# RWKV chunk scan: half of each group's heads cross between the partition halves, so that a product uses all four 64x64 squares of the array

## The chip, the cores and the metric

One core of one Trainium2 chip. The metric is the device time of one launch in microseconds (us). TensorE (PE in the profile) multiplies; VectorE (DVE), ScalarE (ACT) and GpSimd (POOL) work on elements; SyncE (SP) issues most of the loads.

## The reference, cut to what matters

The whole model is several layers; the change touches only the last mixer, an RWKV-7 scan over 16 heads of width 64, run forward and backward over 256 context tokens and 256 latent tokens:

```
S_t = S_{t-1} (diag(w_t) - kk_t^T (a_t * kk_t)) + v_t^T k_t
y_t = S_t r_t
```

All inputs and outputs are float32. `y_t` is wanted for the latent tokens only; each direction starts its latent tokens from the state that its context tokens left.

## The kernel before, in words

The scan goes in chunks of 64 tokens: 8 chunks forward (rounds 0 to 7), then 8 backward (rounds 8 to 15), and round 16 only finishes. Inside a chunk everything is a product of 64x64 blocks, one for each head: cumulated decays (`cum`), the masked products between keys and values (`lta`, `mt`, `rab`), the inverse of a unit triangular matrix by doubling and joining (`n2`, `n3`, `n4`, `p`, `f0`, `m2`, `q2`, `m3`, `q3`), and the values with the state (`w`, `t1`, `t2`, `us`, `s`, `y`). `rab` and `y` exist in latent chunks only (`late`), `s` and `fab` not in the last chunk of a direction (`feeds`).

The 16 heads are in two groups g of 8 heads. A tile of a group is [128, 4, 64]: block a (0 to 3) and partition half i (0 or 1) are a head, so that one tile holds 8 heads. `quarters` issues for one product 8 matmuls (times the number of terms): for each a, half 0 then half 1. Head (a, i) has both operands on partitions 64i to 64i+63, and its result goes to the same half. In the array that is square (0,0) and square (1,1), in turn; squares (0,1) and (1,0) are used by `cum` alone. In the trace each float32 matmul is two MATMUL records with a LDWEIGHTS each, so that a product of 8 matmuls has 16 records.

Each engine runs a generator for each group (`scan_pe`, `scan_act`, `scan_dve`, `scan_pool`). A round has ten steps, one for each yield, here called step 0 to 9. `lead` puts group 0 five steps ahead, and then the two take turns, so that every engine's queue is in a fixed order: step k of group 0, step k-5 (modulo 10) of group 1, and so on. In step 0 of round n stand `cum` of n and `w` of round m = n-1; 1: `t1`; 2: `lta`, `t2`; 3: `n2`, `us`; 4: `n3`, `n4`, `s`, `y`; 5: `p`; 6: `f0`, `m2`; 7: `q2`, `mt`; 8: `m3`, `fab`; 9: `q3`, `rab`. The chunk's own chain goes through all of them; each result is taken out of PSUM by ACT (`BY_ACT`) or DVE before the next step's product reads it. A `Line` makes every instruction of ACT, DVE and POOL wait for the one before it on its engine.

Each group has four of the eight PSUM banks, in rotation over its products (`bank_no`); `T.bank` waits until the product that had the bank four products ago has been taken out.

## Time and profile before

| what | value |
|---|---|
| median of 3 runs | 2984.02 us (2983.59 to 2987.77) |
| the profiled execution, own time | 2979.91 us |
| its span | 2978.1 us |
| mean granted TensorE clock | 0.972 |
| PE busy | 2831.3 us (95%) |
| DVE, ACT, POOL busy | 1742.9, 1296.3, 112.2 us |

A matmul's record lasts from its start to the modelled end of its result, and records overlap; the rate of a stream of matmuls is read from the starts (or from a stretch's length over its count), not from the mean length of a record. The clock is a share of 2.4 GHz, so that 0.50 is the lower level of 1.2 GHz.

### The profile page before, as it was taken

The page shows a single profiled execution, that of the slowest core. Times are in us where ns is not written, and L with a number is a line of the kernel's source. Part 1 is how long each engine was busy: PE and PEld are TensorE (multiplying, and loading weights), DVE is VectorE, ACT ScalarE, POOL GpSimd, SP SyncE. Part 2 cuts the span into 40 slices and gives each one's busy share as a digit, 9 for nine tenths or more (in the row PEclk, how much of TensorE's full clock was granted, in tenths as well). Part 3 has the DMA queues.
Part 4 walks back from the last instruction along what each step waited for, and adds up shares of the span by engine and source line. Part 5 has one row for each costly group of instructions (what it writes and reads, how often), then busy time and mean ns, then how long its engine had stood idle before and what let it go on. Part 6 is the DMA issues. An engine that isn't in the chain of part 4 may idle for free.

```text
span 2978.1 us, 63232 instructions
## 1 busy us (share of the span) xinstructions
PE 2831.3 (95%) x26684; PEld 2314.0 (78%) x26684; DVE 1742.9 (59%) x2702; ACT 1296.3 (44%) x2044; POOL 112.2 (4%) x152
## 2 busy tenths in 40 slices
PE   8999999999999999998989999998999999998998
PEld 7887788888877888676758777784547998985986
DVE  6756667586565765213466877545324564565885
ACT  6645566465555665222435332334104434433333
POOL 0000000000000000000000000000001222220000
PEclk9999999999999999997989999999999999999999
DMA  6554345555543554431001433311210000002443
GB/s 256 187 184 164 134 170 185 180 189 191 188 156 119 186 189 153 176 144 60 2 10 57 169 143 142 120 68 64 99 43 3 5 5 25 5 4 114 156 142 113
DMA packets 50409, 349.72 MB, mean 117 GB/s; under 512 B 5840, under 2 KB 5840, under 8 KB 9808
## 3 DMA queue, kind: packets, MB, share of 16 engines
q1 hardware_dynamic: 49680, 343.56, 32.5%
q8 instruction: 212, 3.47, 0.5%
q0 software_dynamic: 448, 2.11, 0.2%
q14 instruction: 69, 0.57, 0.1%
HBM read 344.61 MB, written 1.05 MB: 116 GB/s over the span
## 4 chain that ended last, share of the span: by engine, by line
PE 82%; DVE 11%; ACT 3%; issue 2%; DMA 1%; DVEq 0%; ACTq 0%; SPq 0%
PE psum L165 81%; DVE arena L98 2%; DVE ring_low L87 2%; DVE arena L87 2%; DVE wide L87 2%; PE psum L170 1%; ACT w_high L144 1%; DVE wide L98 1%; DVE ring L87 1%; DMA ring<-in_evt 1%; ACT wide L138 0%; ACT arena L144 0%; ACT arena L140 0%; ACT L138 0%; DVE small L106 0%
## 5 line engine op out<-in xcount | busy, mean ns | idle before, releaser
L165 PE MATMUL psum<-x_both,w_high 128*128 128x512 f32 (+1 forms) x2800 | 845.1, 374 | 10.4 <-DVE arena L87 8.2
L87 DVE TENSOR_TENSOR ring_low<-ring,w_high 128x2048 fp32r<-128x2048 f32 (+3 forms) x254 | 560.3, 2206 | 427.4 <-ACT w_high L144 412.7
L144 ACT ACTIVATE w_high<-ring 128x2048 fp32r<-128x2048 f32 (+3 forms) x254 | 469.5, 1848 | 528.6 <-PE psum L165 236.5
L165 PE MATMUL psum<-x_both,ring_low 128*128 128x256 f32 (+1 forms) x2104 | 605.3, 301 | 0.0
L165 PEld LDWEIGHTS psum<-x_both,w_high 128*128 128x128 f32 x2800 | 494.9, 190 | 107.2 <-issue 17.6
L165 PE MATMUL psum<-w_high,x_both 128*128 128x512 f32 (+2 forms) x1440 | 451.8, 390 | 10.6 <-issue 10.0
L165 PEld LDWEIGHTS psum<-x_both,ring_low 128*128 128x128 f32 x2104 | 398.3, 189 | 32.5 <-DVE x_both L98 1.4
L165 PE MATMUL psum<-wide,ring 64*64 64x64 f32 (+3 forms) x3888 | 383.6, 272 | 12.4 <-DVE wide L87 7.4
L165 PEld LDWEIGHTS psum<-wide,ring 64*64 64x64 f32 (+2 forms) x3888 | 269.1, 147 | 108.3 <-issue 78.2
L165 PEld LDWEIGHTS psum<-w_high,x_both 128*128 128x128 f32 x1440 | 276.3, 195 | 74.9 <-issue 21.5
L165 PE MATMUL psum<-ring_low,x_both 128*128 128x512 f32 (+2 forms) x720 | 278.7, 387 | 0.0
L144 ACT ACTIVATE arena<-psum 128x256 f32<-128x256 f32 (+1 forms) x341 | 148.4, 435 | 212.3 <-PE psum L165 185.3
L165 PE MATMUL psum<-wide 64*64 64x64 f32 (+3 forms) x5808 | 208.2, 218 | 6.6 <-issue 1.9
L98 DVE SCALAR_TENSOR_TENSOR arena<-arena,prm 128x256 f32<-128x256 f32 x396 | 192.1, 485 | 14.1
L165 PEld LDWEIGHTS psum<-wide 64*64 64x64 f32 (+2 forms) x5808 | 184.7, 133 | 17.8 <-issue 6.8
L165 PE MATMUL psum<-w_high,h_high 128*128 128x512 f32 x440 | 172.4, 392 | 4.1 <-DVE ring_low L87 4.1
L165 PE MATMUL psum<-w_high,h_low 128*128 128x512 f32 x440 | 171.4, 390 | 0.0
L165 PE MATMUL psum<-ring_low,h_high 128*128 128x512 f32 x440 | 171.4, 390 | 0.0
L144 ACT ACTIVATE wide<-psum 128x256 f32<-128x256 f32 (+3 forms) x223 | 102.2, 459 | 146.3 <-PE psum L165 134.5
L87 DVE TENSOR_TENSOR arena<-arena,psum 128x256 f32<-128x256 f32 (+1 forms) x240 | 112.3, 468 | 84.6 <-ACT arena L144 62.7
L165 PEld LDWEIGHTS psum<-ring_low,x_both 128*128 128x128 f32 x720 | 140.8, 196 | 24.9
L165 PE MATMUL psum<-ring,wide 64*64 64x64 f32 (+2 forms) x2016 | 147.5, 238 | 1.5 <-issue 0.8
(201 smaller groups left out, 3022.0 us busy)
## 6 DMA issues: line engine op xcount, KB each, us to landing
ring<-in_f_gu SPq DMA_DIRECT2D x88, 1024.0 KB, 4.9
ring<-in_w_mod SPq DMA_DIRECT2D x48, 1024.0 KB, 4.9
ring<-in_fu SPq DMA_DIRECT2D x44, 1024.0 KB, 4.8
ring<-in_f_dn SPq DMA_DIRECT2D x40, 1024.0 KB, 4.9
ring<-in_w_in SPq DMA_DIRECT2D x28, 1024.0 KB, 4.9
ring<-in_fd SPq DMA_DIRECT2D x20, 1024.0 KB, 4.8
ring<-in_rkvr SPq DMA_DIRECT2D x12, 1024.0 KB, 4.8
ring<-in_w_out SPq DMA_DIRECT2D x8, 1024.0 KB, 5.0
```

The lines of the kernel that those rows point to most:

```text
L87: self.done(self.eng.tensor_tensor(o, a, b, op), then)
L98: self.done(self.eng.scalar_tensor_tensor(out=o, in0=a, scalar=s, in1=b, op0=op0, op1=op1), then)
L144: self.done(self.eng.activation(o, i, ACT.Copy, scale=scale), then)
L165: ins = self.eng.matmul(o, l, r, start=a, stop=z)
L170: ins = self.eng.transpose(o, i, ident[0:i.shape[0], 0:i.shape[0]])
```

## The change

- Blocks a = 0 and 1 of a tile stay as they are. For a = 2 and 3 a product of two operands on half i puts its result on half 1-i (`cross`, `head`). The order is now: squares (0,0), (1,1), (0,1), (1,0), then the same for the next pair of blocks.
- Each cross product moves blocks 2 and 3 to the other half. A product whose inputs and result must have the same side uses the old way (`straight`): `p`, `q3`, one half of `q2`, and the term with the state in `w` and `y`. In `w`, `y` and `q2` it writes to the PSUM bank that a cross product has just written, and PE waits for that one before blocks 2 and 3 (`behind`).
- `n2` gets a third product (the identity minus the near block, turned), because its copy on the other side is now needed; ACT takes three blocks out at once. `it` on DVE is half as wide. `f0` is in `m2`'s banks.
- A product has two banks: blocks 0, 1 in the first, blocks 2, 3 in the second. A group therefore has only two places, chosen by name (`SECOND`), and `T.pair` waits until the product last put there has been taken out.
- `s`, `y`, `mt`, `rab`, `fab` and the moments of the output stand in other steps: `y` in 5, `s` in 6, `rab` in 7, `mt` in 8, `fab` in 9. `pc` is now an Exp on ACT in place of a copy on DVE.
- `value_rows` puts the values into the new layout with the same number of copies.

```diff
+    def pair(self, b, tick):
+        for t in self.taken[b] + tuple(t for t in self.taken[b + 1] if t not in self.taken[b]):
+            self.eng.wait_ge(*t)
+        self.taken[b] = self.taken[b + 1] = (tick,)
 
     def mm(self, o, l, r, a, z, then=None):
...
 
-        STFT, SIT, SUT, SATB, SRAB, SKA, SRH = [[blocks(2) for _ in TWO] for _ in range(7)]
+        SUT = [unit(3).rearrange("p (y k t) -> p y k t", y=3, k=4) for _ in TWO]
+        STFT, SATB, SRAB, SKA, SRH = [[blocks(2) for _ in TWO] for _ in range(5)]
         SE1 = [unit(2)[:, 0:264].rearrange("p (k t) -> p k t", k=4) for _ in TWO]
-        SAL, SBE, SE2, SLT, SMJ, SM4, STD, SMT, SWW, SUS = [[blocks() for _ in TWO] for _ in range(10)]
+        SAL, SBE, SE2, SLT, SMJ, SM4, STD, SMT, SWW, SUS, SIT = [[blocks() for _ in TWO] for _ in range(11)]
         ST = unit(2).rearrange("p (k v) -> p k v", k=8)
 
         MIXES = (4, 2, 1, 5, 0, 3)
...
-        bank_no = [{key: 4 * g + n % 4 for n, key in enumerate(order_of)} for g in TWO]
-
-        def scan_bank(g, key):
-            return bank(bank_no[g][key])
-
-        def single(g, key):
-            return scan_bank(g, key)[:, 0:256].rearrange("p (k t) -> p k t", k=4)
+        SECOND = ("w", "lta", "n2", "n3", "p", "m2", "q2", "m3", "q3")
+
+        def first_bank(g, key):
+            return 4 * g + 2 * (key[1] in SECOND)
+
+        def blocks_of(g, key):
+
+            b = first_bank(g, key)
+            return psum[:, b:b + 2, :].rearrange("p b n -> p (b n)").rearrange("p (k y t) -> p y k t", k=4, y=4)
+
+        def single(g, key, y=0):
+            return blocks_of(g, key)[:, y]
 
         def double(g, key):
-            return scan_bank(g, key).rearrange("p (y k t) -> p y k t", y=2, k=4)
+            return blocks_of(g, key)[:, 0:2]
 
...
@@ -2963,36 +2973,60 @@
             te = T.eng
             al, be, mj, mj4, td, mt, ww, us = [x[g] for x in (SAL, SBE, SMJ, SM4, STD, SMT, SWW, SUS)]
             tt_, tf = STFT[g][:, 0], STFT[g][:, 1]
-            itt = SIT[g][:, 0]
-            uu, tq = SUT[g][:, 0], SUT[g][:, 1]
+            it1 = SIT[g]
+            uu, tq, itt = [SUT[g][:, y] for y in range(3)]
             mm, a_, d_, p_ = sc_mm[g], sc_a[g], sc_d[g], sc_p[g]
 
             def take(key):
-                T.bank(bank_no[g][key], a_[key[0], BY_ACT[key[1]]] if key[1] in BY_ACT else d_[key])
-
-            def quarters(o, terms, then=None):
+                T.pair(first_bank(g, key), a_[key[0], BY_ACT[key[1]]] if key[1] in BY_ACT else d_[key])
+
+            def head(o, l, r, a, i, j, begin, end, then=None):
+
+                p, q = slice(64 * i, 64 * i + 64), slice(64 * j, 64 * j + 64)
+                T.mm(o[q, a, :], l[p, a, :], r[p, a, :] if len(r.shape) == 3 else r[p, :], begin, end, then)
+
+            def cross(o, terms, then=None, open_=False):
+
+                for k, (l, r) in enumerate(terms):
+                    for a in TWO:
+                        end = k == len(terms) - 1 and a == 1 and not open_
+                        for b in (a, a + 2):
+                            for i in TWO:
+                                last = k == len(terms) - 1 and b == 3 and i
+                                head(o, l, r, b, i, 1 - i if b > 1 else i, k == 0 and a == 0, end, then if last else None)
+
+            def straight(o, l, r, begin, then=None, behind=None):
 
                 for a in FOUR:
-                    for k, (l, r) in enumerate(terms):
-                        for i in TWO:
-                            p = slice(64 * i, 64 * i + 64)
-                            T.mm(o[p, a, :], l[p, a, :], r[p, a, :] if len(r.shape) == 3 else r[p, :], k == 0,
-                                 k == len(terms) - 1, then if a == 3 and k == len(terms) - 1 and i else None)
+                    if a == 2 and behind:
+                        te.wait_ge(*mm[behind])
+                    for i in TWO:
+                        head(o, l, r, a, i, i, begin and a % 2 == 0, a % 2 == 1, then if a == 3 and i else None)
 
             def one(key, *terms):
                 take(key)
-                quarters(single(g, key), terms, mm(key))
+                cross(single(g, key), terms, mm(key))
+
+            def one_straight(key, l, r):
+                take(key)
+                straight(single(g, key), l, r, True, mm(key))
+
+            def with_state(key, terms, l):
+                take(key)
+                part = (key[0], key[1] + "v")
+                cross(single(g, key), terms, mm(part), True)
+                straight(single(g, key), l, ST[:, 4 * g:4 * g + 4, :], False, mm(key), part)
 
             def pair(key, first, second):
                 take(key)
-                quarters(double(g, key)[:, 0], [first])
-                quarters(double(g, key)[:, 1], [second], mm(key))
+                cross(single(g, key), [first])
+                cross(single(g, key, 1), [second], mm(key))
 
             for n in ROUNDS:
                 new, old, m = n < 16, n > 0, n - 1
                 ka, rh = SKA[g][:, n % 2], SRH[g][:, n % 2]
...
@@ -3010,7 +3044,7 @@
                     te.wait_ge(*d_[m, "mt"])
                     if m % 8:
                         te.wait_ge(*d_[m - 1, "s"])
-                        one((m, "w"), (mt, values), (SKA[g][:, m % 2], state))
+                        with_state((m, "w"), [(mt, values)], SKA[g][:, m % 2])
                     else:
                         one((m, "w"), (mt, values))
                 yield
...
@@ -3029,53 +3063,61 @@
                 yield
                 if new:
                     te.wait_ge(*d_[n, "tft"])
-                    pair((n, "n2"), (tt_, tf), (tf, tt_))
+                    take((n, "n2"))
+                    cross(single(g, (n, "n2")), [(tt_, tf)])
+                    cross(single(g, (n, "n2"), 1), [(tf, tt_)])
+                    te.wait_ge(*d_[n, "it"])
+                    cross(single(g, (n, "n2"), 2), [(it1, eye)], mm((n, "n2")))
                 if old:
                     te.wait_ge(*a_[m, "t2"])
                     one((m, "us"), (td, ww))
                 yield
-                if new:
-                    te.wait_ge(*d_[n, "it"])
-                    te.wait_ge(*a_[n, "n2"])
-                    one((n, "n3"), (itt, uu))
-                    one((n, "n4"), (uu, tq))
-                if old:
+                if n == 16:
                     te.wait_ge(*d_[m, "us"])
-                    if feeds(m):
-                        te.wait_ge(*a_[m, "fab"])
-                        one((m, "s"), (SATB[g][:, 1], values), (SATB[g][:, 0], us))
-                    if late(m):
-                        te.wait_ge(*d_[m, "rab"])
-                        one((m, "y"), (SRAB[g][:, 1], values), (SRH[g][:, m % 2], state), (SRAB[g][:, 0], us))
-                yield
-                if n == 16:
-                    for _ in range(5):
+                    te.wait_ge(*d_[m, "rab"])
+                    with_state((m, "y"), outputs, SRH[g][:, m % 2])
+                    for _ in range(6):
                         yield
                     return
+                te.wait_ge(*a_[n, "n2"])
+                one((n, "n4"), (uu, tq))
+                one((n, "n3"), (itt, uu))
+                yield
                 te.wait_ge(*a_[n, "n4"])
                 te.wait_ge(*d_[n, "n3"])
-                one((n, "p"), (tq, SIT[g][:, 1]))
+                one_straight((n, "p"), tq, it1)
+                if old and late(m):
+                    te.wait_ge(*d_[m, "us"])
+                    te.wait_ge(*d_[m, "rab"])
+                    with_state((m, "y"), outputs, SRH[g][:, m % 2])
                 yield
                 te.wait_ge(*d_[n, "p"])
-                one((n, "f0"), (tf, eye))
                 te.wait_ge(*p_[n, "mj1"])
-                one((n, "m2"), (mj, tf))
+                take((n, "m2"))
+                cross(single(g, (n, "m2"), 1), [(tf, eye)])
+                cross(single(g, (n, "m2")), [(mj, tf)], mm((n, "m2")))
+                if old and feeds(m):
+                    te.wait_ge(*d_[m, "us"])
+                    te.wait_ge(*a_[m, "fab"])
+                    one((m, "s"), (SATB[g][:, 1], values), (SATB[g][:, 0], us))
                 yield
                 te.wait_ge(*a_[n, "m2"])
-                pair((n, "q2"), (uu, tt_), (tt_, uu))
+                take((n, "q2"))
+                cross(single(g, (n, "q2"), 1), [(tt_, uu)], mm((n, "q2v")))
+                straight(single(g, (n, "q2")), uu, tt_, True, mm((n, "q2")), (n, "q2v"))
                 te.wait_ge(*p_[n, "br"])
-                one((n, "mt"), (be, ka))
+                if late(n):
+                    pair((n, "rab"), (al, rh), (be, rh))
                 yield
                 te.wait_ge(*d_[n, "q2"])
                 te.wait_ge(*p_[n, "mj2"])
                 one((n, "m3"), (mj, tf))
+                one((n, "mt"), (be, ka))
+                yield
+                te.wait_ge(*a_[n, "m3"])
+                one_straight((n, "q3"), uu, tt_)
                 if feeds(n):
                     pair((n, "fab"), (al, eye), (be, eye))
-                yield
-                te.wait_ge(*a_[n, "m3"])
-                one((n, "q3"), (uu, tt_))
-                if late(n):
-                    pair((n, "rab"), (al, rh), (be, rh))
                 yield
...
@@ -3128,20 +3170,21 @@
                 se.wait_ge(*mm[key])
                 A.copy(o, single(g, key), a_(key), scale=scale)
 
-            def take_both(o, key):
-                se.wait_ge(*mm[key])
-                A.copy(o, double(g, key), a_(key))
-
             for n in ROUNDS:
                 new, old, m = n < 16, n > 0, n - 1
                 if n == 8 and g == 0:
                     decay_act(A, 1)
                 if new:
+                    z = n // 8
+                    pc = PC[:, 8 * (n % 2) + 4 * g:8 * (n % 2) + 4 * g + 4]
                     se.wait_ge(*mm[n, "cum"])
                     if old:
-                        se.wait_ge(*d_[m, "pc"])
+                        se.wait_ge(*d_[m, "ak"])
                         se.wait_ge(*p_[m, "br"])
                     A.act(e1[:, :, 1:65], single(g, (n, "cum")), ACT.Exp, a_((n, "e1")))
+                    if n > 1 and feeds(m - 1):
+                        se.wait_ge(*d_[m - 1, "s"])
+                    A.act(pc, single(g, (n, "cum"))[:, :, 0 if z else 63], ACT.Exp)
                     A.act(e2, single(g, (n, "cum")), ACT.Exp, a_((n, "e2")), scale=-1.0)
                 if old:
                     take(ww, (m, "w"))
...
+                se.wait_ge(*mm[n, "m2"])
+                A.copy(STFT[g][:, 0], single(g, (n, "m2"), 1))
+                A.copy(uu, single(g, (n, "m2")), a_((n, "m2")), scale=-1.0)
                 yield
                 yield
                 take(uu, (n, "m3"), -1.0)
+                yield
                 if feeds(n):
-                    take_both(SATB[g], (n, "fab"))
-                yield
+                    se.wait_ge(*mm[n, "fab"])
+                    A.copy(SATB[g], double(g, (n, "fab")), a_((n, "fab")))
...
@@ -3196,7 +3242,7 @@
                     z, c = n // 8, chunk(n)
                     ge.wait_ge(*a_[n, "e2"])
                     if n:
-                        ge.wait_ge(*mm[m, "rab" if late(m) else "q3"])
+                        ge.wait_ge(*mm[m, "fab" if feeds(m) else "q3"])
                     G.tt(SBE[g], K[:, hs, 64 * c:64 * c + 64], SE2[g], ALU.mult, None if late(n) else p_((n, "br")))
                     if late(n):
...
@@ -3238,59 +3301,25 @@
                 if new:
                     z, c = n // 8, chunk(n)
                     tok = slice(64 * c, 64 * c + 64)
-                    pc = PC[:, 8 * (n % 2) + 4 * g:8 * (n % 2) + 4 * g + 4]
                 yield
                 if new:
                     ve.wait_ge(*a_[n, "e2"])
                     D.tt(SAL[g], AK[:, hs, tok], e2, ALU.mult)
                     D.tt(SKA[g][:, n % 2], KK[:, hs, tok], e1[:, :, 2 * z:2 * z + 64], ALU.mult, d_((n, "ak")))
-                    D.copy(pc, e1[:, :, 1 if z else 64], d_((n, "pc")))
                 yield
                 if new:
                     ve.wait_ge(*mm[n, "lta"])
                     D.tt(tft, double(g, (n, "lta")), over(near[:, z:z + 2, :]), ALU.mult, d_((n, "tft")))
-                    D.tt(it, PAIR, tft, ALU.subtract, d_((n, "it")))
+                    D.tt(it1, EYES, tft[:, 1], ALU.subtract, d_((n, "it")))
                 yield
                 if old:
                     ve.wait_ge(*mm[m, "us"])
...
@@ -3303,20 +3332,41 @@
                     yield
                     yield
                     return
-                yield
+                ve.wait_ge(*mm[n, "n3"])
+                D.tt(it1, it1, single(g, (n, "n3")), ALU.add, d_((n, "n3")))
+                yield
+                ve.wait_ge(*mm[n, "p"])
+                D.tt(tft[:, 1], it1, single(g, (n, "p")), ALU.add, d_((n, "p")))
+                if old and late(m):
+                    outputs(m)
+                elif old and m < 8 and g == 0:
+                    D.tsc(BV[:, m, :], BV[:, m, :], lx[:, 1, m:m + 1], None, ALU.add, None)
+                yield
+                if old and feeds(m):
+                    ve.wait_ge(*mm[m, "s"])
+                    po = bc(PC[:, 8 * (m % 2) + 4 * g:8 * (m % 2) + 4 * g + 4], 64)
+                    if m % 8:
+                        D.tt(s4, s4, single(g, (m, "s")), ALU.add)
+                        D.tt(s4, s4, po, ALU.mult, d_((m, "s")))
+                    else:
+                        D.tt(s4, single(g, (m, "s")), po, ALU.mult, d_((m, "s")))
                 yield
                 ve.wait_ge(*mm[n, "q2"])
                 D.tt(tft, tft, double(g, (n, "q2")), ALU.add, d_((n, "q2")))
-                ve.wait_ge(*mm[n, "mt"])
-                D.tt(SMT[g], single(g, (n, "mt")), bm(ms[:, z, :], 4), ALU.mult, d_((n, "mt")))
-                yield
-                yield
-                ve.wait_ge(*mm[n, "q3"])
-                D.tt(STD[g], tft[:, 0], single(g, (n, "q3")), ALU.add, d_((n, "q3")))
                 if late(n):
                     ve.wait_ge(*mm[n, "rab"])
                     D.tt(SRAB[g], double(g, (n, "rab")), mi[:, z, :].unsqueeze(1).unsqueeze(1).to_broadcast([128, 2, 4, 64]),
                          ALU.mult, d_((n, "rab")))
+                yield
+                ve.wait_ge(*mm[n, "mt"])
+                D.tt(SMT[g], single(g, (n, "mt")), bm(ms[:, z, :], 4), ALU.mult, d_((n, "mt")))
+                if m >= 12:
+                    moments(m)
+                elif old and late(m) and m < 8 and g == 0:
+                    D.tsc(BV[:, m, :], BV[:, m, :], lx[:, 1, m:m + 1], None, ALU.add, None)
+                yield
+                ve.wait_ge(*mm[n, "q3"])
+                D.tt(STD[g], tft[:, 0], single(g, (n, "q3")), ALU.add, d_((n, "q3")))
                 yield
 
...
```

## Rows read from the trace of the kernel before

**Rows 1.** Windows over the scan: busy time, clock, DMA.

```profile
core 0: us, PE busy (x) PEld busy (x) DVE busy (x) ACT busy (x) POOL busy (x), PEclk, DMA share, GB/s
2259.00:2265.00 6.00, 4.54 (x76) 4.20 (x78) 1.30 (x3) 1.36 (x3) 0.81 (x1) 0.50 0.00 0
2300.00:2324.00 24.00, 23.51 (x773) 22.95 (x772) 13.93 (x28) 10.09 (x25) 6.32 (x9) 1.00 0.02 5
2348.70:2360.14 11.44, 11.41 (x384) 11.27 (x384) 7.35 (x14) 4.96 (x12) 3.59 (x5) 1.00 0.02 5
2348.70:2372.90 24.20, 24.02 (x802) 23.61 (x802) 15.22 (x29) 10.07 (x25) 7.43 (x11) 1.00 0.02 5
2401.20:2429.50 28.30, 27.98 (x930) 27.43 (x930) 17.13 (x32) 10.08 (x25) 7.39 (x11) 1.00 0.02 4
2447.20:2467.40 20.20, 20.19 (x240) 12.06 (x240) 3.90 (x8) 7.58 (x13) 0.82 (x1) 1.00 0.01 2
...
2496.70:2519.60 22.90, 22.62 (x754) 22.23 (x754) 11.75 (x23) 10.05 (x24) 6.30 (x9) 1.00 0.02 5
...
2592.60:2623.40 30.80, 28.18 (x928) 27.48 (x928) 19.45 (x39) 10.42 (x25) 9.04 (x12) 1.00 0.01 4
2623.40:2655.60 32.20, 29.62 (x928) 28.93 (x928) 18.88 (x38) 10.06 (x24) 7.59 (x10) 0.95 0.02 4
2655.60:2687.00 31.40, 30.24 (x976) 29.15 (x976) 19.17 (x39) 10.85 (x25) 6.13 (x8) 1.00 0.01 4
...
2690.00:2702.00 12.00, 8.27 (x186) 6.45 (x182) 8.85 (x22) 1.58 (x5) 0.00 (x0) 1.00 0.01 3
```

**Rows 2.** The chain that ended last, 2250 to 2730, by line.

```profile
by line: PE psum L165 80.6%; DVE wide L87 5.7%; DVE ring L87 3.7%; issue 2.3%; DVE small L106 1.3%; DMA ring<-in_rwo 1.1%; DVE ntmp L87 0.9%; DVE wide L98 0.8%; ACT wide L144 0.7%; ACT wide L138 0.7%; ACT L138 0.5%; ACT ring L138 0.4%; ACT 
```

**Rows 3.** Timeline of PE in a round: start, length, count.

```profile
2303.03 1.10 PE L165 MATMUL psum<-wide 64*64 64x64 f32 x32
2303.97 0.63 PE L165 MATMUL psum<-wide,ring 64*64 64x64 f32 x16
```

**Rows 4.** Timeline of PE in an earlier mixer (GLA): other small products.

```profile
1440.29 0.46 PE L165 MATMUL psum<-wide 64*32 64x32 f32 x32
...
1442.20 0.73 PE L165 MATMUL psum<-wide 64*32 64x16 f32 x64
...
1444.74 0.76 PE L165 MATMUL psum<-wide 64*32 64x32 f32 x64
```

**Rows 5.** Groups of PE by form over the whole span: count, busy us, mean ns.

```profile
L165 PE MATMUL psum<-wide 64*64 64x64 f32 x4864 | 193.4, 221 | 6.6 <-issue 1.9 <-DVE ring L87 1.6 <-ACT wide L144 1.5
...
L165 PE MATMUL psum<-wide 64*32 64x32 f32 x640 | 8.0, 201 | 0.0
```

**Rows 6.** Timeline of all engines: how a result is handed over.

```profile
2566.06 0.38 ACT L144 ACTIVATE ring<-psum 128x256 f32<-128x256 f32 x1
...
2566.50 0.68 PE L165 MATMUL psum<-ring 64*64 64x64 f32 x16
...
2567.23 0.38 ACT L144 ACTIVATE ring<-psum 128x256 f32<-128x256 f32 x1 [0.78 <-PE psum L165]
```

**Rows 7.** Groups by form in rounds 1 to 7, 2277 to 2447: DVE, then ACT.

```profile
L87 DVE TENSOR_TENSOR wide<-psum,cx 128x512 f32<-128x512 f32 x20 | 13.8, 692 | 8.0 <-PE psum L165 7.3
L87 DVE TENSOR_TENSOR wide<-wide,psum 128x256 f32<-128x256 f32 x27 | 11.4, 421 | 18.7 <-PE psum L165 17.3
...
L144 ACT ACTIVATE wide<-psum 128x256 f32<-128x256 f32 x54 | 20.7, 383 | 18.9 <-PE psum L165 15.8
...
L144 ACT ACTIVATE wide<-psum 128x512 f32<-128x512 f32 x26 | 15.5, 597 | 13.6 <-PE psum L165 12.6
```

**Rows 8.** Timeline of DVE: group 1's `SAL`, `SKA`, `pc`, beside POOL's work.

```profile
2311.74 0.86 DVE L87 TENSOR_TENSOR ring<-wide,ring 128x256 f32<-128x256 f32 x1
2312.63 1.00 DVE L87 TENSOR_TENSOR wide<-wide,ring 128x256 f32<-128x256 f32 x1
2313.67 0.58 DVE L102 COPY small<-ring 128x4 f32<-128x4 f32 x1
```

96 lines of the change are left out of this document (39 added, 57 removed).

## The prediction

> **What bounds the kernel now.** I read the windows over the scan first. In a round without `rab` and `y` PE is busy 98% of the time, and one half round holds 384 records in 11.44 us; latent rounds hold 930 records in 28.3 us [rows 1]. The chain that ended last is 81% PE there, DVE about 13% [rows 2]. So the scan is bound by the number of matmuls that PE gets through, except in the last rounds, which hold as many records (928) but take 32.2 us, because DVE also makes the moments (18.9 us busy) [rows 1].
>
> How fast PE gets through them is read from starts: 32 records from 2303.03 to 2303.97, 29.4 ns each [rows 3], with a record 221 ns long [rows 5]. Matmuls alternate between two squares, so that each square takes one every 58.7 ns.
>
> **What a matmul costs with four squares.** The trace has no 64x64 blocks on all four squares. The nearest row: 32 records of 64x32 that go round four squares (two row halves by two column places) take 0.46 us, 201 ns of it the last one's length [rows 4, 5]: 0.26/31 = 8.4 ns each, 33 ns for each square. With eight squares the rate is the same (0.76 us for 64: 8.9 ns). So four squares do run beside each other, halves shared by row and by column included, and PE can start a record with its weight load at least every 9 ns. A square's own period is 58.7 ns for 64 columns. Bounds: 14.7 ns a record (58.7/4) if the squares are independent, 29.4 ns if nothing is gained. I take 14.7, the end that the nearest row supports.
>
> The Trainium skill ("TensorE: Matmul & The Clock Gate", Back-to-back issue gap) says that start-to-start never falls below about 25 ns however small the product; the 8.4 to 8.9 ns of [rows 4] disagree. By that rule a cross record would cost 25 ns; that is rival D.
>
> **PE's work.** Per group and plain round before: 192 matmuls (half round: 384 records x 29.4 ns = 11.3 us; seen 11.44 [rows 1]). After: 200, as `n2` gets 8 more. 40 stay on two squares (`cum`, `p`, `q3`, half of `q2`, the state's term of `w`), 160 cross. Half round: 80 x 29.4 ns + 320 x 14.7 ns = 2.35 + 4.70 = 7.06 us. A latent one adds `y` (16 cross, 8 straight) and `rab` (16 cross): 8.47 us against 13.6. If PE stayed the bound, a plain round would fall from about 23.3 to 14.1 us and the scan by some 150 us. It won't, because the others don't get faster.
>
> **The other engines.** DVE is busy 13.9 of 24 us in a plain round, with 28 instructions [rows 1]. `pc` leaves it (up to 0.58 us each [rows 8]), and `it` shrinks from 0.69 to 0.42 [rows 7]: 12.6 us are left, and with some 0.06 us between dependent instructions 14 us, as much as PE. ACT gets `pc` (about 0.2 us) and a third block in `n2` (0.60 + 0.21 us); `f0` moves with `m2` at no change. POOL has 6 of 24 us [rows 1] and hides. Loads: none is moved, the DMA share is 0.02. The Trainium skill says so too ("TensorEngine Tiling (Array Packing)", PSUM Bottleneck): a faster array leaves the taking out of PSUM as the bound; DVE's row agrees.
>
> **The chain, walked.** With both near 14 us, what counts is the chain: product, result out, next product. A result can be taken 0.25 us after its last record starts, and the next product starts 0.06 us after ACT or DVE ends (2566.44 to 2566.50; 2566.96 to 2567.23) [rows 6]. ACT takes 0.38 (256 columns) and 0.60 (512), DVE 0.42 and 0.69 [rows 7]. Cross products take PE 0.24 us, straight ones 0.47. Queues are in order, group 0's step before group 1's. A plain half round, from `p` of group 0 (step 5):
> - 0 to 0.5 `p`, DVE has it out at 1.2. `cum` of group 1 to 0.9, its three Exps 1.2 to 2.3, `w` to 1.7 (0.1 of it waiting for the bank that its cross part wrote), out at 2.7.
> - `m2` and `s` of group 0 on PE from 1.7 to 2.7; ACT is behind the Exps and `w` and has `m2` out at 3.6; DVE has the state at 3.9. Only then can DVE do group 1's `SAL` and `SKA` (0.86 + 1.00 beside POOL [rows 8]): 5.85. `q2` is done by 4.7, but its DVE work stands behind them: 5.85 to 6.6.
> - `lta` 5.9 to 6.4, DVE's mask to 7.35, then ACT's copy to 7.8. `n2` now waits for that copy, as it has the same place: 7.85 to 8.6, three blocks out at 9.6. `m3` is out at 8.7.
> - `q3` 8.8 to 9.3, `fab` to 9.7, `n4` to 10.0; ACT takes `fab` to 10.6. `cum` of group 0 shares its place with `fab`: 10.65.
> The other half, with `SAL` and `SKA` at 0.42 each, comes to 9.2 us. Together 19.8, and 0.5 for some nine restarts in which the weight load too must wait (0.055 us before its matmul): 20.3 us, PE busy some 70%.
>
> A latent round: `y` lengthens step 5 by 1.0 us of PE and delays the Exps; `rab` puts 0.7 us of DVE before the mask, and `mt` waits for it: 1.3 to 1.9 us per half, 23.4 us in all. With moments DVE needs 2.0 us more before `us` or `n3`, of which 1.2 per half show: 25.8.
>
> **The sum.** Rounds before [rows 1]: four plain ones from 22.9 to 24.0, 23.3 on average; four with one of `rab` or `y`, 24.6 on average (the 24.20 is one); two latent, 28.3; three with moments, 30.8 to 32.2, 31.5 on average.
> - 4 plain windows: 4 x 3.0 = 12
> - 4 with one of the two, to 21.3: 4 x 3.3 = 13
> - 2 latent: 2 x 4.9 = 10
> - 3 with moments: 3 x 5.7 = 17
> - first round, the end of each direction, the start of the second, the tail: by their records (438, 576, 848, 280), 2.5 + 3 + 4 + 1 = 11
> - the second direction's decay products (240 records, 20.2 us [rows 1]): 0. `value_rows`: same copies, 0. `s` one or two steps later: it is wanted by `w` four steps on, 0; if its cover went, 0.9 us a half.
> Sum 63 us. The profiled execution: 2979.9 - 63 = 2917. The median stands 4.1 above it: 2984.0 - 63 = 2921.
>
> **Rivals.**
> A, the above: 2900 to 2944. Chance 0.58.
> B, the two places per group and the fixed order cost more than I walked: each of the ten turns of a round loses another 0.25 us, as every product must wait for the last but one to be out, where it had four banks. For it: `lta` before `n2`, `fab` before `cum`, `rab` before `mt`, `d_s` before `rab`. Against: mostly the chain waits for these anyway. 16 x 2.5 = 40 us given back: 2961; range 2944 to 2972. 0.18.
> C, slower: no more than two 64x64 squares run beside each other, since two weight loads of 64 columns on one row half, or two results into one column half, take turns. Then 400 records per half instead of 384 cost 0.5 us, and the waits inside `w`, `q2` and `y` 0.3: 1.6 a round, 25 in all: 3009. It decides from a cross record of 26 ns on: (11.65 - 2.35 - 0.9 of stalls)/320. Against it, the four squares of [rows 4]; for it, that these were 32 columns wide. 0.07.
> D, a floor of 25 ns on starts: half round 2.35 + 8.0 + 0.65 = 11.0, 1.3 a round: 2964. 0.04.
> E, the clock: PE is busy 70% instead of 98%, and it drops to 1.2 GHz in parts. At 0.50 PE was busy 4.54 of 6 us at the scan's start, but at 69% (8.27 of 12) it held 1.00 [rows 1]. A half round of PE work would be 14.1 us at the lower level: 8 us a round more than 20.3. A third of the time there gives 43 back: 2964; at half of it the gain is gone. 0.05, of which 0.02 slower.
> F, the stalls overlap better than walked: 2875 to 2900. 0.05.
> G, the parts cancel: 2984. 0.03.
>
> **How the numbers follow.** What this kernel's measurement can tell from no change is 0.2%, 6 us. Faster: A, B, D, F and 0.03 of E: 0.88. Same: 0.03. Slower: 0.09. The range leaves out G, C, E's slow part, and most of F: 2893 to 2970. A's own is 2900 to 2944.
>
> **What would show it.** Cross products: 16 records in 0.24 us, starts 15 ns apart; 29 ns is C, 25 is D. PE busy about 70 to 80% of the scan, DVE about 65%, and a plain round near 20.3, a latent one near 23.4. Waits of PE for ACT before `n2` and `cum`, for DVE before `lta`. The granted clock at 1.00 after the first round, or not (E). 512 more small records than before (16 for each of 32 group-rounds). Wrong would make it above all a rate between 15 and 29, or a chain whose turns take longer than walked.

## The result, and the profile after

| | us | against before |
|---|---|---|
| before, 4 runs beside it | 2984.32 (2983.59 to 2987.77) | |
| after, 4 runs | 3007.22 (3004.56 to 3012.05) | 1.0076 [1.0059, 1.0094] |
| predicted | 2921 (2893 to 2970) | faster, with a chance of 0.88 |

The kernel after is 23 us slower. The forecast was wrong in sign and lay 86 us off. The two profiled executions, 3012.05 and 2979.91 us, lie 32 us apart. 28 of these are in the scan: 492.8 us before and 520.8 after, from the first `cum` to the first product of the output. 6 lie ahead of it, where both programs are the same, and behind it the kernel after makes up 2.

The page of the kernel after: the row of PE in its first part, of the instruction queue in its third, and the shares by engine of the chain that ended last. The page of the kernel before has 2831.3 us (95%) and 26684 records for PE, and 212 packets on the instruction queue.

```profile
PE 2746.7 (91%) x27196; PEld 2209.3 (73%) x27196; DVE 1718.3 (57%) x2670; ACT 1309.7 (44%) x2076; POOL 110.4 (4%) x152
...
q8 instruction: 216, 3.54, 0.5%
...
PE 75%; DVE 14%; issue 5%; ACT 5%; DMA 1%; DVEq 0%; POOL 0%; ACTq 0%; SPq 0%; POOLq 0%
```

PE has 512 records more, as counted beforehand, and is busy 85 us less, yet the end comes later: PE now stands idle, and 5% of the chain is "issue", time in which the engine waited for nothing that the profile shows.

Windows over the scan (us, PE, PEld, DVE, ACT and POOL busy with their counts, clock, DMA share, GB/s). They answer to [rows 1]. First 100 us of the kernel before, then the kernel after:

```profile
2300.00:2400.00 100.00, 98.96 (x3286) 97.16 (x3284) 59.94 (x115) 40.26 (x97) 27.53 (x38) 1.00 0.02 5
```

```profile
2300.00:2325.30 25.30, 18.22 (x800) 16.36 (x800) 11.15 (x24) 10.84 (x26) 5.81 (x8) 0.97 0.02 4
...
2350.00:2400.00 50.00, 34.55 (x1618) 31.60 (x1609) 23.65 (x48) 21.02 (x51) 13.13 (x18) 1.00 0.02 4
2300.00:2400.00 100.00, 69.41 (x3166) 63.20 (x3167) 45.80 (x94) 42.32 (x102) 25.06 (x34) 0.99 0.02 4
...
2600.00:2700.00 100.00, 71.89 (x3106) 66.67 (x3103) 52.26 (x106) 36.99 (x89) 24.29 (x33) 0.93 0.02 4
```

A plain round is 800 records. It took 25.3 us, where 23.3 us had stood before and 20.3 us had been forecast. PE is busy 69 to 72%, about as forecast (70 to 80%), at a granted clock of 0.97 to 1.00 in the first rounds and 0.93 in the last. DVE is busy 44 to 46% there and 52% in the last rounds, not 65%. So no engine is full. The count of records tells more: 3166 in 100 us, 31.6 ns each, where the kernel before gets 3286 into the same 100 us, 30.4 ns each, with PE 99% busy. The array works half as long on a crossing product, and the records pass no faster. In the second direction (2490 to 2700) the two are level: 6498 records after, 6421 before.

What the lower clock cost: between 2280 and 2700 the kernel after had the lower level for 27 us, the kernel before for 3. In these stretches (the decay products of the second direction left out) its records came every 35.9 ns, elsewhere every 31.9, which makes some 3 us of the 28.

The chain after, 2250 to 2730, by line; it answers to [rows 2]:

```profile
by line: PE psum L170 53.4%; issue 22.2%; DVE wide L87 7.4%; DVE ring L87 6.9%; ACT wide L144 4.5%; ACT wide L138 1.2%; ACT ring L144 0.9%; ACT ring L138 0.9%; POOL ring L150 0.7%; ACT small L138 0.5%; DVE small L106 0.4%; ACT L138 0.3%; PE
```

"issue" has risen from 2.3% to 22.2%, DVE and ACT have grown too, PE fell from 81% to 53%. Timeline of PE after, some of the rows from 2302 to 2316 (start, length, count, idle time before and what ended it); it answers to [rows 3]:

```profile
2302.34 0.63 PE L170 MATMUL psum<-cx,ring 64*64 64x64 f32 x30
2302.82 0.69 PE L170 MATMUL psum<-wide 64*64 64x64 f32 x32
...
2304.62 0.50 PE L170 MATMUL psum<-cx,wide 64*64 64x64 f32 x10 [0.53 <-issue]
...
2308.61 0.40 PE L170 MATMUL psum<-ring,wide 64*64 64x64 f32 x13 [0.58 <-issue]
...
2312.49 0.21 PE L170 MATMUL psum<-wide 64*64 64x64 f32 x1 [0.89 <-issue]
...
2313.01 0.68 PE L170 MATMUL psum<-wide,ring 64*64 64x64 f32 x32
...
2316.14 0.51 PE L170 MATMUL psum<-cx,ring 64*64 64x64 f32 x19 [0.76 <-issue]
```

Two things are to be seen. The crossing products do run at the forecast rate: 30 records in 0.63 us and 32 in 0.68 or 0.69, less the last one's 0.22, are 14 to 15 ns each (2313.01: 0.46/31 = 14.8 ns). And PE stands still without any semaphore just before 2304.62, 2308.61, 2312.49 and 2316.14, 3.7 to 4.0 us apart. Between two such stops lie 125 or 126 records in the trace, and some records can be missing. The stops fall in the middle of products, not only ahead of one.

The view of waits, PE, 2230 to 2740 (us in total, times, longest); first before, then after:

```profile
PE psum L165 <- DVE wide L87: 9.7, 10, 2.3
...
PE psum L165 <- issue: 2.8, 5, 0.9
```

```profile
PE psum L170 <- issue: 93.2, 91, 3.4
PE psum L170 <- DVE ring L87: 14.4, 30, 1.3
PE psum L170 <- ACT wide L144: 13.1, 32, 1.3
```

Idle time without a semaphore: 93.2 us after against 2.8 before. Idle time for ACT, DVE and POOL, all rows of that view added: 45 against 18. Groups by form after, 2277 to 2447, for [rows 7] and [rows 8]:

```profile
L144 ACT ACTIVATE wide<-psum 128x768 f32<-128x768 f32 x13 | 10.5, 811 | 11.0 <-PE psum L170 10.9
...
L138 ACT ACTIVATE small<-psum 128x4 f32<-128x4 f32 x13 | 2.3, 174 | 1.1
```

```profile
L87 DVE TENSOR_TENSOR ring<-cx,wide 128x256 f32<-128x256 f32 x12 | 5.1, 425 | 0.4
```

These terms came as forecast: three blocks out in 0.81 us (0.60 + 0.21), `pc` on ACT 0.17, `it` 0.425.

**Theory F, formed on this trace** (not to be mixed up with the prediction's rival F)**.** PE's instructions come into the engine as packets of 16 KB on the instruction queue. Here is that queue, 2300 to 2400, before and then after:

```profile
q8 instruction: 27, 0.44, 1.7%
```

```profile
q8 instruction: 25, 0.41, 1.7%
```

27 packets for 3286 records, 25 for 3166: one packet for 122 to 127 records, and as many stand between two stops of PE. A packet is 16.4 KB (3.54 MB by 216), which spread over 128 records with their 128 weight loads is 64 bytes for each of 256 instructions. The stops go with the packets: in the DMA records packets start at 2302.32, 2306.07, 2309.84 and 2313.84, and the four stops above end 2.30 to 2.65 us after each. In the trace's DMA records no two packets start less than 3.33 us apart, over the whole execution, in either kernel and in any of those below; the median in the scan is 3.87 us before and 4.03 after. F says: over a longer stretch PE can't get 128 records in less than about 3.5 us, 27 ns a record. Before, two squares needed 128 x 29.4 ns = 3.76 us for them, and the supply just hid behind the array. After, the array would be through with 128 crossing ones in 1.9 us and with an average mix in 2.3 (400 in 7.06), and PE stands until the next packet is in. The Trainium skill ("Runtime: NRT & Kernel Launch", Instruction fetch mechanics) says that an engine's instructions are refilled in 16 KiB blocks of 256, and that the cost of crossing from one block to the next is "mostly hidden". The trace agrees with the size; in this scan the cost isn't hidden.

Rivals: R1, the stops are waits after all (the order, the two places for each group, the split products); R2, long runs on four squares disturb each other, or gain nothing.

### The profile page after: what moved, and what is told of

Same layout as the page of the kernel before. It is cut to its first block, busy times and chain, and to the rows that moved or that the text cites. A ratio compares the mean times of both kernels' runs of the same rounds, so it can differ in the third digit from the quotient of the medians.

```text
span 3010.2 us, 64207 instructions
## 1 busy us (share of the span) xinstructions
PE 2746.7 (91%) x27196; PEld 2209.3 (73%) x27196; DVE 1718.3 (57%) x2670; ACT 1309.7 (44%) x2076; POOL 110.4 (4%) x152
## 3 DMA queue, kind: packets, MB, share of 16 engines
q8 instruction: 216, 3.54, 0.5%
## 4 chain that ended last, share of the span: by engine, by line
PE 75%; DVE 14%; issue 5%; ACT 5%; DMA 1%; DVEq 0%; POOL 0%; ACTq 0%; SPq 0%; POOLq 0%
PE psum L170 74%; DVE arena L98 3%; DVE ring_low L87 2%; DVE arena L87 2%; DVE wide L87 2%; DVE ring L87 1%; PE psum L175 1%; ACT wide L138 1%; ACT w_high L144 1%; ACT wide L144 1%; DVE wide L98 1%; ACT arena L144 0%; ACT arena L140 0%; DVE arena L94 0%; ACT wide L140 0%
## 5 line engine op out<-in xcount | busy, mean ns | idle before, releaser
L170 PE MATMUL psum<-wide,ring 64*64 64x64 f32 (+3 forms) x3888 | 343.1, 282 | 32.2 <-issue 17.2
L170 PEld LDWEIGHTS psum<-wide,ring 64*64 64x64 f32 (+2 forms) x3888 | 225.0, 153 | 133.5 <-issue 98.4
L170 PE MATMUL psum<-wide 64*64 64x64 f32 (+3 forms) x5296 | 144.5, 224 | 46.7 <-issue 26.0
L144 ACT ACTIVATE wide<-psum 128x256 f32<-128x256 f32 (+4 forms) x223 | 109.2, 490 | 167.8 <-PE psum L170 157.6
L170 PEld LDWEIGHTS psum<-wide 64*64 64x64 f32 (+2 forms) x5296 | 121.6, 135 | 63.8 <-issue 38.8
L170 PE MATMUL psum<-ring,wide 64*64 64x64 f32 (+2 forms) x2528 | 140.1, 244 | 21.8 <-issue 20.2
```

Of the source, the lines that this page charges most:

```text
L144: self.done(self.eng.activation(o, i, ACT.Copy, scale=scale), then)
L170: ins = self.eng.matmul(o, l, r, start=a, stop=z)
```

## The experiments

Each is timed against the kernel before on the same chip; a gain or loss against the kernel after goes by the two ratios.

**1. Streams of products on PE alone.** In the kernel before, ahead of the scan:

```diff
+for cols, places in ((64, ((0, 0), (1, 1), (0, 1), (1, 0))), (64, ((0, 0), (1, 1))), (16, ((0, 0), (1, 1), (0, 1), (1, 0)))):
+    for n in range(384):
+        i, j = places[n % len(places)]
+        p = slice(64 * i, 64 * i + 64)
+        T.mm(bank(4 + (i != j))[64 * j:64 * j + 64, 0:cols], eye[p, :], eye[p, 0:cols], True, True)
```

> The kernel before, with three streams of 384 float32 products of the identity put in ahead of the output's work, on PE alone, results unused: 64x64 on four squares in turn, 64x64 on two squares, 64x16 on four squares. Each stream is 768 records, that is six stretches of 128 records, and 128 records are the 256 instructions that one 16 KB packet of the instruction queue brings. Theory F (PE's instructions arrive in such packets, and no faster than one in about 3.5 us, the shortest interval between packets in the traces of before and after): all three streams take about the same, 6 x 3.5 = 21 us, 27 ns a record, with a stop of PE without a semaphore about once in 128 records, in the first and the third stream. Theory R1 (the stops of the kernel after are waits for ACT and DVE) and my prediction: the streams have no such waits, so they take 768 x 14.7 ns = 11.3 us, 768 x 29.4 ns = 22.6 us, and about 768 x 8.6 ns = 6.6 us. Theory R2 (long runs on four squares disturb each other): the first is slower than 11.3 us evenly, by the record, and the third is not near the second.

Measured: 3050.82 us, one run, 68 us above the kernel before (2982.63). The timeline of PE over the three streams. The first stream's 768 records end in the sixth row. That row's last 24 are already the second stream's, at the pace of two squares, and the last 24 of the row of 768 are the third's:

```profile
2252.99 2.44 PE L165 MATMUL psum<-cx 64*64 64x64 f32 x152 [1.08 <-DVE wide L87]
2256.44 2.10 PE L165 MATMUL psum<-cx 64*64 64x64 f32 x128 [1.01 <-issue]
2259.91 2.10 PE L165 MATMUL psum<-cx 64*64 64x64 f32 x128 [1.38 <-issue]
2263.93 3.50 PE L165 MATMUL psum<-cx 64*64 64x64 f32 x128 [1.92 <-issue]
2267.68 2.10 PE L165 MATMUL psum<-cx 64*64 64x64 f32 x128 [0.25 <-issue]
2271.42 2.43 PE L165 MATMUL psum<-cx 64*64 64x64 f32 x128 [1.65 <-issue]
2275.44 22.83 PE L165 MATMUL psum<-cx 64*64 64x64 f32 x768 [1.59 <-issue]
2298.46 2.06 PE L165 MATMUL psum<-cx 64*64 64x16 f32 x128 [0.19 <-issue]
2301.93 14.30 PE L165 MATMUL psum<-cx 64*64 64x16 f32 x512 [1.42 <-issue]
```

Windows over the first stream, over its second to fifth burst, and over the second stream from 2275.44 on:

```profile
2252.99:2272.98 19.99, 13.79 (x768) 13.05 (x770) 0.12 (x2) 0.77 (x1) 0.00 (x0) 0.91 0.02 4
2256.44:2271.42 14.98, 9.78 (x512) 9.19 (x513) 0.00 (x0) 0.00 (x0) 0.00 (x0) 0.89 0.02 4
2275.44:2297.68 22.24, 22.10 (x741) 21.82 (x742) 0.00 (x0) 0.00 (x0) 0.00 (x0) 1.00 0.02 4
```

And the DMA view from 2252.99 to 2275.44, in 40 slices of 0.56 us, with the queue's row:

```profile
GB/s 0 29 0 0 0 0 0 0 29 0 0 0 0 0 0 29 0 0 0 0 0 29 0 0 0 0 0 0 29 0 0 0 0 0 0 29 0 0 0 0
...
q8 instruction: 6, 0.10, 1.6%
```

This is the mechanism in the open. Nothing waits for a semaphore, and on four squares PE does 128 records in 2.10 us (14.8 ns each, less the last one's 0.22), stands 1.0 to 1.9 us, and does the next 128. (One burst took 3.50 us, at a granted clock of 0.54; the stop after it shrank to 0.25.) The first stream took 20.0 us, where F wanted 21 and the array alone needs 11.3. Its first burst was 152 records long; from the second to the fifth it is 512 records in 14.98 us, 29.3 ns each. A packet starts at 2254.01, 2257.59, 2261.58, 2265.07, 2269.17 and 2273.11; PE goes on 2.25 to 2.61 us after each, and the next packet starts 1.14 to 1.69 us after that. The interval between packets is these two added; why the next one doesn't start sooner, no run shows. On two squares 744 records take 22.25 us (2275.44 to 2297.69), 29.9 ns each, with no stop longer than 0.3 us between starts. So four squares are worth 2% in a long stream of float32 products, not 50%. R1 has no waits to point to here. R2 fails too: within a packet the rate is the full one.

The third stream tells less than it was meant to. From 2298.46 on 128 of its records ran like those of the first stream (2.06 us, then 1.42 of standing). With that stop the granted clock fell to the lower level, and it stayed there to the stream's end at 2319, though PE was busy nearly all the time from then on:

```profile
2298.46:2301.90 3.44, 2.05 (x128) 1.95 (x128) 0.00 (x0) 0.00 (x0) 0.00 (x0) 0.98 0.02 5
2301.90:2305.40 3.50, 3.47 (x128) 3.47 (x129) 0.00 (x0) 0.00 (x0) 0.00 (x0) 0.50 0.02 5
```

At 0.50 128 records need 3.5 us anyway, just what the packets allow, and the stops shrink to 0.4 us and less.

**2. The order of after on two squares.** `head(o, l, r, b, i, i, ...)` in place of `1 - i if b > 1 else i`, and `value_rows` as before.

> The kernel after, with its order, its two places for each group, its third product in n2 and its splitting of w, y and q2, but with every product on the two straight squares as before (and value_rows as before). Theory F: the scan can't go faster than its instructions arrive, and these are as many as in the kernel after; a record on two squares takes 29.4 ns against some 27 ns for the instructions, so this comes out near the kernel after, 0 to 25 us above it: 3007 to 3032. Theory R1: the order and the places cost what is lost, four squares gain on top of that: the array's time grows by 320 x 14.7 ns = 4.7 us a half round, at least half of it on the chain, 32 x 2.4 us = 75 us or more above the kernel after: 3080 or more. Theory R2 (four squares are no gain at all in this mix): equal to the kernel after within 6 us.

Measured: 3015.00 us, 1.0108 [1.0093, 1.0123]. Windows and PE's waits:

```profile
2300.00:2400.00 100.00, 95.04 (x3083) 92.95 (x3081) 48.04 (x96) 40.55 (x98) 24.47 (x34) 1.00 0.02 4
```

```profile
PE psum L170 <- issue: 9.9, 19, 1.8
```

As F had it: PE is 95% busy again, its stops are gone (9.9 us), and the time is only 8 us above that of after, where R1 wanted 75. This run also splits the result. The new order and the 512 records cost 32 us on two squares: 512 x 29.4 ns = 15 us of array. The other 17 are a remainder that no run splits; the waits inside `w`, `q2`, `y` and for the two places are the candidates. In PE's view of waits (2230 to 2740) its idle time is 31 us here against 21 before, 7 of the 10 without a semaphore. Four squares give 8 to 10 us of the 32 back. R2's "equal within 6 us" is missed by little, and it was the stream that settled R2.

**3. Fewer records at the same array time.** In after, `s`, `mt`, `rab` and `fab` for blocks 0 and 1 alone. The products of blocks 2 and 3 are left out, so the result isn't the reference's:

```diff
-                        for b in (a, a + 2):
+                        for b in (a,) if half else (a, a + 2):
```

> The kernel after, but s, mt, rab and fab are computed for two of the four heads of a partition half alone (those of the two straight squares; their results are taken for the crossing heads too). A product on four squares and its half on two squares take PE's array the same time, so the array's time and the chain of waits are those of the kernel after; what is gone is 1408 records, 11 stretches of 128. rab and fab leave PSUM by two instructions in place of one. Theory F: 11 packets fewer at 3.5 us each, 38 us less than the kernel after, less what waits take their place: 2967 to 2985. Theories R1 and R2: within 8 us of the kernel after, rather above it.

Measured: 2971.28 us, 0.9956 [0.9940, 0.9973]: 36 us below after, 25 ns for each record left out. PE's waits:

```profile
PE psum L170 <- issue: 51.2, 65, 2.1
PE psum L170 <- DVE ring L87: 24.2, 36, 1.5
```

The array's time (by 29.4 ns for each straight record and 14.7 for each crossing one) and the order are those of after, and only the supply of instructions is relieved: idle time without a semaphore falls from 93.2 to 51.2 us.

**4. Half the records for each product.** The scan's tiles in bfloat16, in after and in before:

```diff
-        spare = [[x, 0] for x in [wide[:, 25344:33024]] + [ring[:, i, :] for i in range(3)]]
+        scan_low = at("scan_low", [128, 15360], WHIGH + 25344, BF16)
+        spare = [[scan_low[:, :], 0]]
```

> The kernel after with the scan's tiles and a copy of the identity held in bfloat16, so that each product of the scan but cum is one weight load and one matmul record in place of two of each; order, places, waits and the instructions of ACT, DVE and POOL are the same. Half of PE's scan instructions are gone and so is half of the array's time; the chain of waits is left as it was. Theory F (instructions arrive at 27 to 29 ns a record): the stops of PE vanish, and the rounds come down to the chain that the prediction walked (20.3 us a plain round, in place of the 23 to 24 that 800 records at 29 ns take): 40 to 90 us below the kernel after, 2917 to 2967. Theory R1 (the stops are waits in the order and the two places): the chain's waits stay, only the short products shrink, 32 half rounds x at most 0.5 us: 2990 to 3007.

> The kernel before with the same edit (bfloat16 tiles in the scan, one record of each kind for a product). Theory F: this kernel too is then free of its instructions, and of the two squares as well, since a product's time on the array falls with its records; what is left is DVE's work and the chain, with pc and the larger it on DVE: 30 to 90 us below the kernel before, within 20 us of after_half. Theory R1: about 2920 as well, so that after_half comes out 60 us or more above this one.

Measured: after_half 2899.64 us, 0.9719 [0.9704, 0.9733]; before_half 2892.06 us, 0.9690 [0.9674, 0.9706]. Windows of after_half, two plain rounds and a bit (a round is 416 records now), and PE's waits:

```profile
2300.00:2324.00 24.00, 14.82 (x516) 11.80 (x509) 16.87 (x32) 13.19 (x34) 7.91 (x11) 0.50 0.01 3
2324.00:2348.00 24.00, 15.55 (x530) 12.74 (x531) 15.76 (x31) 13.51 (x32) 7.62 (x11) 0.50 0.01 3
```

```profile
PE psum L171 <- DVE scan_low L88: 64.6, 106, 2.4
PE psum L171 <- ACT scan_low L145: 52.1, 111, 1.9
...
PE psum L171 <- issue: 4.1, 4, 2.1
```

The stops without a semaphore are gone (4.1 us), and what is left is the chain, with its shorter products: 24 x 416/516 = 19.3 and 24 x 416/530 = 18.8 us a round, where I had walked 20.3 for float32. R1, which left the stops as waits, is 90 us off. after_half went 17 us below its expected range, which had been worked out from the walk's 20.3, and before_half 2 us below its own. The four squares with the new order show no gain here either: before_half is 8 us faster. Part of that can be the clock's. In the profiled execution of after_half the second direction's decay products, 16 pairs of 64x512, ran at the lower level, a pair every 1.71 us; in before_half they ran at the upper one, a pair every 0.86 us, which is 14 us less for work that is the same. In the two plain rounds, both at 0.50, before_half is ahead by less: a round is 400 records there, 18.2 to 18.6 us by the same two windows. With PE busy 62 to 65% the granted clock was 0.50 in these rounds of after_half. That is what rival E had feared for the kernel after, where it came about for 27 us only: at 69% busy it kept 0.99 from 2300 to 2400.

**5. As many records as before.** POOL makes the third block of `n2` out of the masked tile:

```diff
-                    te.wait_ge(*d_[n, "it"])
-                    cross(single(g, (n, "n2"), 2), [(it1, eye)], mm((n, "n2")))
+                    G.tt(o[:, 0:2], EYES[:, 0:2], t[:, 0:2], ALU.subtract)
+                    for j in TWO:
+                        q = slice(64 - 64 * j, 128 - 64 * j)
+                        G.tt(o[64 * j:64 * j + 64, 2:4], EYES[q, 2:4], t[q, 2:4], ALU.subtract, p_((n, "itt")) if j else None)
```

> The kernel after, but the transposed inverse's first factor comes from three POOL instructions (identity minus the lower block, two of them across the partition halves) instead of n2's third product on PE: 512 records fewer, so as many as the kernel before, and ACT takes 512 columns instead of 768 out of n2's place. Theory F: four packets of instructions fewer, 4 x 3.6 us = 14 us less than the kernel after: 2993, range 2988 to 2998. Theory R1: PE's third product stands beside nothing else, 0.24 us of PE and 0.2 us of ACT in each of 32 steps, at most 10 us, and POOL's 1.2 us can put it back: 2997 to 3010. The two differ little here; it is a check on the size of the term, not on the cause.

Measured: 2983.49 us, 1.0005 [0.9990, 1.0019]. 512 records fewer gave 21 us by the ratios, more than F's 14 (4 packets) and than R1's 10, and the time lies below both ranges. ACT's copy of 512 instead of 768 columns (0.2 us, on the chain in each half round) fits the rest, but wasn't run alone. With as many records as the kernel before, it takes the kernel before's time. The four squares' gain and what is left of the new order's cost cancel, as I read it.

**6. Fewer records than before.** With itt_pool as the base, three versions join products: `cum` with 128 columns of weights (itt_cum: 256 records fewer), `be` and `al` with 128 moving columns (joined: 704 fewer), and both (fewer: 960 fewer).

```diff
-                            T.mm(o[64 * i:64 * i + 64, a, :], LW[r, c // 2, f:f + 64], tri2[r, z, 0:64], True, True,
+                        T.mm(o[:, a, :], LW[r, c // 2, f:f + 128], tri2[r, z, 0:64], True, True,
...
-                one((n, "mt"), (be, ka))
+                    twin((n, "mt"), 0, be, EY_AT, KA_AT + z, mm((n, "mt")))
```

> itt_pool, and besides: cum's products with 128 columns of weights in place of two of 64 (256 records fewer), and products with the same weights joined into one with 128 moving columns (be with the keys and the identity, al and be with the queries and the identity: 704 records fewer). The result is that of the reference. 1472 records fewer than the kernel after, 960 fewer than the kernel before; the array does the same sums. Theory F: 11.5 packets of instructions fewer, at the 25.6 ns a record that the half-sided kernel showed 38 us, at 29 ns 43 us below the kernel after: 2964 to 2970, so 0.5% below the kernel before. Theory R1: the array's time is unchanged and the extra orderings between ACT and DVE on one place come on top: 3000 to 3020.

> itt_pool, with cum's products on 128 columns of weights (256 records fewer) and nothing else: the step between itt_pool (2983.5) and fewer (2977.3). Theory F: 256 x 27 ns = 7 us below itt_pool: 2976 to 2979. If so, the joined products of fewer gained nothing more for their 704 records, and what they add (ACT and DVE taking turns on one place) ate it. If this is 2982 or more, cum's records lie where PE has its instructions anyway, and the gain of fewer is that of the joined products.

> fewer without its change to cum: itt_pool with the joined products, 704 records fewer than itt_pool and 1216 fewer than the kernel after, no 64x128 weights. Theory F: 704 x 27 ns = 19 us below itt_pool (2983.5): 2964, range 2960 to 2972, and so below fewer as well, because cum is short again. If it stays within 5 us of itt_pool, the waits in the order (ACT and DVE taking turns on one place) have taken the place of the missing instructions.

Measured: fewer 2977.30 us, 0.9973 [0.9958, 0.9988]; itt_cum 2985.04, 1.0005 [0.9991, 1.0019]; joined 2981.63, 0.9989 [0.9975, 1.0004]. All three miss what F's bare count gives. Below itt_pool, at 27 ns a record: 26 us for fewer and 10 found (by the ratios), 7 and none for itt_cum, 19 and 5 for joined. For `cum` the reason is in the trace of the next kernel. For the joined products it stays open. PE's idle time without a semaphore is hardly lower than itt_pool's:

```profile
PE psum L170 <- issue: 69.4, 83, 1.8
```

itt_pool has 75.5. The expectation's other reading, that waits for ACT and DVE take the place of the missing instructions, isn't borne out: these rows, with POOL's, add up to 49 us, in itt_pool to 50. A rival is the clock. The profiled execution of joined (2988.15 us) had the lower level all through the second direction's decay products:

```profile
2447.00:2482.00 35.00, 34.11 (x219) 16.86 (x223) 1.90 (x5) 8.61 (x15) 0.73 (x1) 0.51 0.13 46
```

PE is busy throughout and doesn't wait for instructions. The 16 records of 64x512 against a constant are spread over 24.7 us there, from the first start to the last, and over 12.4 in itt_pool at the upper level: 12 us. The twelve executions of joined lie between 2970.35 and 2990.78 us, and the four fastest, up to 2976.15, had mean granted clocks of 0.966 to 0.969, the four slowest 0.961 to 0.964. So part of the missing gain can be the clock; no run tried it apart.

**7. What bounded the kernel before.** Two squares, same order; `cum` with 128 columns of weights, and in `s` and `fab` one product with 128 moving columns in place of two heads' products (the second head's is left out, so the result isn't the reference's):

```diff
+                            x = (r[p, a, :] if len(r.shape) == 3 else r[p, :]).unsqueeze(1).to_broadcast([64, 2, 64])
+                            T.mm(o[p, a:a + 2, :], l[p, a, :], x, k == 0, k == len(terms) - 1,
```

> The kernel before (two squares), with 1152 records fewer at the same array time and in the same order: cum's products take 128 columns of weights in place of two of 64, and in s and fab one product with 128 moving columns stands for two with 64 (it computes the first head's result of each pair twice, so the second head's is left out). Theory A, my prediction's reading of the kernel before (PE's array on two squares sets the pace, 29.4 ns a record): the array's work is unchanged, so is the time: within 6 us of the kernel before, 2978 to 2990. Theory F in its strong form (the instructions set the pace in the kernel before too, the array just behind them): up to 1152 x 27 ns = 31 us less: 2953 to 2975.

> before_wide without its change to cum: 896 records fewer than the kernel before, the same array time, no 64x128 weights. In before_wide cum took 1.03 us in place of 0.47 (2314.85 to 2315.88 in its trace), 32 times 0.56 = 18 us, which hid what the fewer records gave. Theory A (the array on two squares sets the pace before): 2978 to 2990. Strong form of theory F (the instructions set it): 896 x 27 = 24 us less, 2960 to 2970.

Measured: before_wide 2997.00 us, 1.0041 [1.0023, 1.0058]; before_wide64 2976.31, 0.9967 [0.9954, 0.9980]. PE in before_wide around a `cum`:

```profile
2302.26 1.10 PE L165 MATMUL psum<-cx,wide 64*128 64x64 f32 x8
2303.29 0.33 PE L165 MATMUL psum<-wide,ring 64*64 64x64 f32 x4
```

Eight records with 64x128 weights hold PE from 2302.26 to 2303.29. The eighth starts at 2303.09, which is 119 ns from one start to the next, where sixteen with 64x64 weights take 0.47 us [rows 3]. 32 times 0.56 us is 18 us, near the 22 us that lie between the two ratios, and enough to eat the 256 records' 7 us in itt_cum. The Trainium skill ("TensorEngine Tiling (Array Packing)", Key Properties) says that a change of the tiling mode drains TensorE. That may be part of it, but the row shows more than a drain at each end, since all eight come slowly, 111 to 160 ns apart.

before_wide64 has the answer: 896 records fewer give 8 us, not none (A) and not 24 (F alone). About half of the 8 is the array's, whose time was not quite the same. A `fab` of before_wide64, and the product after it:

```profile
2309.26 1.04 PE L165 MATMUL psum<-cx,ring 64*64 64x128 f32 x16
2310.13 1.32 PE L165 MATMUL psum<-wide 64*64 64x64 f32 x36
```

A record with 128 columns takes 0.87/16 = 54.4 ns, two with 64 take 58.8: 896 x 4.4 ns = 4 us less. The array set the pace of the kernel before, as I had read it, with the supply of instructions right behind it: a packet's 3.5 us under the array's 3.76.

## Why the prediction was wrong, step by step

- **The rate on four squares: right.** 14.8 ns a record, against 14.7. Rivals C (29.4 ns, 26 ns and more to decide for it) and D (25 ns) are wrong in their mechanism; that C's 3009 is close to 3007 is chance.
- **PE's work in a half round: this step failed.** "4.70 us" for 320 crossing records and 7.06 for a half round was the array's time taken for PE's. It rested on "PE can start a record with its weight load at least every 9 ns", which the 32 and 64 records of [rows 4] show and which I carried over to 400 in a row. Those bursts are shorter than the 128 records of a packet. Over longer stretches a record on four squares cost 29 ns on average (experiment 1), 27 by the shorter intervals between packets, so that a half round needs 400 x 27 to 29 ns = 11 to 12 us instead of 7, and the kernel took 12.6. In the kernel before the bound could be read: its 212 packets on the page, 27 of them in 100 us, each for 128 records, and never under 3.34 us apart. I had looked at the loads ("none is moved") and not at the queue that brings the instructions.
- **`n2`'s 16 records more for each group-round** were counted, but as 0.24 us of the array. They are 4 packets, 14 to 15 us by the interval of packets, and itt_pool's 21 us hold them beside ACT's smaller copy.
- **The chain walked: not what bound the scan.** 20.3 us a plain round; with the instructions halved, and shorter products, it was 18.8 to 19.3. That is near, but no run shows the float32 chain by itself.
- **`pc`, `it`, the third block, decay products:** as forecast. DVE was busy 44 to 52%, not 65%, because the rounds were longer. The clock did drop, as rival E has it, but for 27 us of 420 and at some 3 us.
- **Rival B** (the order and the two places) can be real in kind: 17 us are left for it on two squares. My C had 25 us for these and the 16 records, and two_squares showed 32.
- **The balance:** new order and 512 records +32 us, four squares -8 to -10: +23. The gain of four squares didn't vanish into one new wait. It was bounded by the 2 to 7% between the array's time for 128 records and the packets' (2% in the streams, 3.76 against about 3.5 us by the shorter intervals). PE's waits for ACT, DVE and POOL (18 us before, 45 after) now come beside its stops.

A version faster than both is at hand in two forms: with the reference's result in float32 by a little (fewer, 0.9973), and with the scan's tiles in bfloat16, so with less precision, by 3% (before_half, 0.9690), on two squares.

## What to carry to other kernels

Count PE's instructions beside its array time. Here a float32 64x64 product is four of them (two weight loads and two records), and once the array's time for 256 instructions came near 3.5 us, a faster array gave little more; fewer instructions gave up to 25 ns a record (experiment 3), and less where the clock or other waits stood in the way (experiment 6). A rate read from a burst holds for a burst's length; before it is carried to a stage, look for the longest stretch in which the trace shows it, and at the interval of the instruction packets. Idle time marked "issue" that recurs after an equal number of instructions, in the middle of products, was that supply here and no semaphore. And read the granted clock of every stage before a difference of 10 us is given to an edit.

## What the runs showed of the hardware that was not expected

- PE's instruction packets: 16 KB, never under 3.33 us apart in thirteen profiled executions, PE going on 2.25 to 2.61 us after a packet's start (stream).
- 64x16 products on four squares come every 14.6 ns a record (stream: 128 from 2298.46 to the last start at 2300.31), 64x64 ones every 14.8: no faster for a quarter of the columns.
- 64x128 weights in a row on one row half: 119 ns a record (before_wide), against 29.4 for 64x64 on two squares.
- The granted clock stayed at 0.50 in the stream of 64x16 products with PE busy 3.47 of 3.50 us, and in the bfloat16 scans with PE busy 62 to 79%; it was 0.99 in the kernel after at 69%.
- The second direction's decay products, the same work in every kernel, took twice as long at the lower level: 24.7 against 12.4 us from the first to the last of the 16 records of 64x512 against a constant (joined and after_half; itt_pool and before_half).
